# Attention slots of a two-layer trunk: the place of the division by the softmax sum, and of the convolution's taps

## The chip, the core and the metric

The kernel runs on one core of one Trainium2 chip, in one launch. The metric is the device time of an execution in microseconds. TensorE (PE) multiplies matrices and turns blocks, VectorE (DVE), ScalarE (ACT) and GpSimd (POOL) work on elements, and SyncE (SP) starts the transfers of the weights. Every engine has its own queue and works through it in the order of the program; semaphores tie the queues together. An instruction that waits holds up all that stands behind it in its queue.

## What is computed

Two layers, each with token mixing in three branches, a LayerNorm, and a SwiGLU network with a second LayerNorm, for 512 tokens of 1024 numbers in float32. Cut to what matters here:

```python
h = x @ w_in                                    # split into column groups
# branch A: 8 heads, one shared key; a light indexer picks 128 keys of each query
s = (q . k) * scale; s = where(selected, s, -inf)
y_a = softmax(s) @ v
# branch B: 8 heads with keys of their own, causal softmax over 512 keys
y_b = softmax(where(causal, (q . k) * scale, -inf)) @ v
# branch C: a causal depthwise convolution of width 31 over 512 channels
h = conv(a * sigmoid(g), width=31) + conv_b; y_c = silu(layer_norm(h))
gates = sigmoid(gate_pre + b_gate)              # 3 x 1024 columns of x @ w_in
merged = gates[0]*(y_a @ wb[0]) + gates[1]*(y_b @ wb[1]) + gates[2]*(y_c @ wb[2])
x = layer_norm(ALPHA * x + merged @ w_out)
```

## The kernel before, in words

A product in float32 is made of three: every operand is split into a high part, rounded to the format that TensorE takes, and a low part, the remainder, and high times high, high times low and low times high are summed. ScalarE makes the high part as a copy, VectorE or GpSimd the low part as a difference. That holds for the weights (`high` at L526 on ScalarE, `low` at L453 on GpSimd) and for everything inside attention.

The change touches one stretch of each layer, the function `attention`, which every engine has in its own version. It works through 64 *units* in a layer (`UNITS`), a unit being one head and one block of 128 queries. Units 0 to 31 are branch B, 32 to 63 branch A. Unit n has n mod 4 as its query block, and its scores are 128 times that block plus one wide, so 128, 256, 384 or 512 columns. The masked scores of unit n lie in `pbuf[n % 3]`. Time is cut into *slots*. In slot s:

- TensorE makes the scores of unit s (`score`, L962 to L970), turns the probabilities of unit s - 2 block by block (`turn`, L936), and in every second slot multiplies two turned units by the values (`value`, L986). Between these it works on the projections of the three gates: 24 weight tiles of eight *parts* (three products of 512 columns each, L829 to L831), dealt evenly over the slots by `attention_steps`. A turn waits for `prob_ready`.
- VectorE masks the scores and takes their extreme (`mask`, L1283), makes the reciprocal of a unit's sum (`inverse`, L1290), adds two halves of a value product (`combine`, L1305, odd slots), and takes the low part of the turned probabilities (`turned_lows`, L1297), for which it waits for ScalarE's copy of the same block. Beside these it has the 124 *taps* of the convolution (4 blocks of channels by 31, L1315 to L1321), each a pass over 512 columns that adds to a PSUM bank, and in slots 0 to 11 two of the selection steps of branch A (L1265, L1267). The table `TAPS_AT` says how many taps a slot has. The first tap of a slot stands ahead of `turned_lows`, all others behind it.
- ScalarE makes the exponential of unit s with its sum (`exponentials`, L564), divides (`probabilities`, L571: it multiplies by the reciprocal), copies turned probabilities out of PSUM (`turned_probabilities`, L580), copies half a value product (`value_part`, L587), makes the sigmoid of a finished gate tile (`gate`, L530, at a tile's last part) and the high part of a coming weight tile (L526, at a tile's first part). Some slots (`PREP`) hold the preparation of a head: two turned copies (L552, L553, or L556 and L558). Slot 8 has the copies of the shared key and value (L613, L614), slots 57 to 60 one copy each of the finished branch B (L621).

The order of each queue is written out by hand: ScalarE and TensorE walk over the same list `STEPS`, VectorE has its own loop over the slots. In ScalarE's walk, the step ("turn", s - 2) of slot s holds three instructions: the copy of unit s - 2, the exponential of unit s, the division of unit s - 1. In VectorE's loop a slot begins with the mask of unit s, and the reciprocal of unit s - 1 follows.

Of the kernel before, what the change touches and what calls it, by code (L numbers as in the profile page):

```python
# [108 lines left out]
UNITS = 2 * AH * NT  # L109
# [7 lines left out]
Y_SPLIT = {57 + c: c for c in range(4)}  # L117
KA_SLOT = 8
# [4 lines left out]
KEEP_SLOT = len(SELECT_LATE) // 2  # L123
TAPS_AT, _taps = [], 0
for _slot in range(UNITS):
    _n = 1 if _slot <= KEEP_SLOT else 3 if (_slot - KEEP_SLOT) % 5 == 4 else 2
    TAPS_AT.append(range(_taps, min(_taps + _n, CK * CW)))
    _taps = TAPS_AT[-1].stop
assert _taps == CK * CW
# [109 lines left out]
def build(nc, x_t, ple_t, pos, freq, weights, params, out):  # L239
    with ExitStack() as ctx:  # L240
# [270 lines left out]
        def _(act):  # L511
# [20 lines left out]
            def attention(layer, first):  # L532
# [57 lines left out]
                for kind, n in STEPS:  # L590
                    if kind == "part" and n[1] == 0:
                        high(T_GATE + n[0] + LEAD, first)
                    elif kind == "part" and n[1] == DK - 1:
                        g, j = GATE_ORDER[n[0]]
                        gate(T_GATE + n[0], first, 6 + n[0] % 2, gate_at(g, j), column("bg", g * DK + j), gate_done)
                    elif kind == "rope":
                        rope_keys()
                    elif kind == "prep":
                        prepare(n)
                    elif kind == "turn":  # L600
                        turned_probabilities(n)
                        if n + TURN_LAG < UNITS:
                            exponentials(n + TURN_LAG)
                        if n + 1 < UNITS:
                            probabilities(n + 1)
                    elif kind == "score" and n < TURN_LAG:
                        exponentials(n)
                        if n == 1:
                            probabilities(0)
                    elif kind == "value":  # L610
                        value_part(n)
                    elif kind == "slot" and n == KA_SLOT:
                        nc.scalar.activation(ka_h[:], ka_t[:], ACT.Copy).then_inc(ka_high, 1)  # L613
                        nc.scalar.activation(idx_r[:, :, G_VA - AD:G_VA], h_idx[:, :, G_VA:G_VA + AD],  # L614
                                             ACT.Copy).then_inc(va_high, 1)
                    elif kind == "slot" and n in Y_SPLIT:
                        c = Y_SPLIT[n]
                        if c == 0:
                            act.wait_ge(turn_out, turns + (TURN_AT[("prep", ("A", 3), "")] + 1))
                            act.wait_ge(value_out, layer * PAIRS + PAIRS // 2)  # L620
                        nc.scalar.activation(yh[1][:, c], yb[:, c], ACT.Copy).then_inc(y_high, 1)  # L621
# [43 lines left out]
            for layer in range(L):  # L665
# [87 lines left out]
                for q in range(12):  # L753
# [8 lines left out]
                    if q >= 8:  # L762
                        for c in range(2):
                            n = 2 * (q - 8) + c
# [423 lines left out]
        def _(dve):  # L1188
# [80 lines left out]
            def attention(layer, last_conv_input):  # L1269
# [84 lines left out]
                steps.wait()  # L1354
                last_conv_input()
                for slot in range(UNITS + NORM_LAG):
                    if slot < UNITS:
                        mask(slot)
                    if 1 <= slot <= UNITS:
                        inverse(slot - 1)  # L1360
                    if slot >= NORM_LAG and (slot - NORM_LAG) % 2:
                        combine((slot - NORM_LAG) // 2)
                    taps = list(TAPS_AT[slot]) if slot < UNITS else []
                    late = SELECT_LATE[2 * slot:2 * slot + 2]
                    for k in taps[:1]:
                        tap(k)
                    for step in late[:1]:
                        select(step, back=0)
                    if slot in PREP:
                        lows("prep", PREP[slot])  # L1370
                    if TURN_LAG <= slot < UNITS + TURN_LAG:
                        turned_lows(slot - TURN_LAG)
                    for k in taps[1:]:
                        tap(k)
                    for step in late[1:]:
                        select(step, back=0)
                    if KEEP_SLOT <= slot < KEEP_SLOT + NT - 1:
                        qt = slot - KEEP_SLOT + 1
                        span = slice(wide(qt), wide(qt) + width(qt))
                        steps.wait()  # L1380
                        steps.done(v.tensor_scalar(keep_bias[:, span], work[:, span], -2e38, NEG, ALU.is_gt, ALU.mult))
                    if slot == KA_SLOT:
                        dve.wait_ge(ka_high, layer + 1)
                        v.tensor_tensor(ka_l[:], ka_t[:], ka_h[:].bitcast(F32), ALU.subtract).then_inc(ka_ready, 1)
                        dve.wait_ge(va_high, layer + 1)
                        v.tensor_tensor(idx_r[:, :, G_VA:G_VA + AD], h_idx[:, :, G_VA:G_VA + AD],
                                        idx_r[:, :, G_VA - AD:G_VA].bitcast(F32), ALU.subtract).then_inc(va_low, 1)
# [412 lines left out]
```

## Time and profile before

| | us |
|---|---|
| median of 3 runs | 1850.85 |
| lowest and highest run | 1849.95, 1851.07 |
| the profiled execution, whole | 1852.88 |
| its span, first to last instruction | 1851.1 |
| TensorE busy | 1811.0 |
| VectorE busy | 1065.1 |
| ScalarE busy | 813.2 |
| GpSimd busy | 771.2 |

The profile is of one execution; times in it count from its first instruction. Matmuls overlap in the queue, and their ends are modelled, so TensorE counted as busy may still lose time; its weight loads (PEld) are the better sign of a wait. "Idle before" an instruction is the time for which its engine did nothing, with the engine, tile and line whose signal ended it. Where two instructions of one engine overlap by some 0.1 us, the next has begun while the end of the last is still being written. The attention stretch of the first layer runs from about 157 to 373 us, that of the second from about 1073 to 1289 us.

### The profile page before, as it was taken

The page shows a single profiled execution, that of the slowest core. Times are in us where ns is not written, and L with a number is a line of the kernel's source. Part 1 is how long each engine was busy: PE and PEld are TensorE (multiplying, and loading weights), DVE is VectorE, ACT ScalarE, POOL GpSimd, SP SyncE. Part 2 cuts the span into 40 slices and gives each one's busy share as a digit, 9 for nine tenths or more (in the row PEclk, how much of TensorE's full clock was granted, in tenths as well). Part 3 has the DMA queues.
Part 4 walks back from the last instruction along what each step waited for, and adds up shares of the span by engine and source line. Part 5 has one row for each costly group of instructions (what it writes and reads, how often), then busy time and mean ns, then how long its engine had stood idle before and what let it go on. Part 6 is the DMA issues. An engine that isn't in the chain of part 4 may idle for free.

```text
span 1851.1 us, 25182 instructions
## 1 busy us (share of the span) xinstructions
PE 1811.0 (98%) x8654; PEld 1502.9 (81%) x8654; DVE 1065.1 (58%) x1965; ACT 813.2 (44%) x1431; POOL 771.2 (42%) x336
## 2 busy tenths in 40 slices
PE   9999999999999999999999999999999999999997
PEld 9887787878778888888897877888887888888885
DVE  6379999868973111203254999997889711111033
ACT  4544777743433232322244457777434322322222
POOL 5443223345354444444444522233543544444541
PEclk9999999999999999999999999999999999999998
DMA  5322111223233332333333321122232332333331
GB/s 185 103 95 88 46 58 58 70 69 103 82 112 102 91 101 92 101 103 103 101 95 91 108 75 46 58 64 63 83 103 79 112 100 93 94 99 101 103 103 57
DMA packets 47032, 166.04 MB, mean 90 GB/s; under 512 B 5472, under 2 KB 5728, under 8 KB 46944
## 3 DMA queue, kind: packets, MB, share of 16 engines
q1 hardware_dynamic: 46080, 163.60, 28.3%
q10 hardware_dynamic: 864, 1.28, 0.2%
q8 instruction: 54, 0.88, 0.2%
q14 instruction: 34, 0.28, 0.0%
HBM read 162.76 MB, written 2.10 MB: 89 GB/s over the span
## 4 chain that ended last, share of the span: by engine, by line
PE 69%; issue 12%; DVE 9%; POOL 5%; ACT 4%; DMA 0%; DVEq 0%; POOLq 0%; ACTq 0%; SPq 0%
PE banks L829 18%; PE banks L831 18%; PE banks L830 18%; POOL sb_wl L453 4%; PE banks L880 3%; PE banks L882 3%; PE banks L881 3%; PE banks L936 2%; PE banks L986 2%; DVE sb_work L1267 1%; DVE sb_top L1265 1%; ACT sb_pbuf L564 1%; ACT sb_pbuf L571 1%; ACT sb_wh L526 1%; DVE banks L1319 1%
## 5 line engine op out<-in xcount | busy, mean ns | idle before, releaser
L453 POOL TENSOR_TENSOR sb_wl<-sb_wraw,sb_wh 128x1024 fp32r<-128x1024 f32 x303 | 743.8, 2458 | 1039.1 <-ACT sb_wh L526 1038.8
L829 PE MATMUL banks<-sb_xh,sb_wh 128*128 128x512 f32 x1344 | 540.6, 402 | 2.8 <-POOL sb_wl L453 1.8
L831 PE MATMUL banks<-sb_xh,sb_wl 128*128 128x512 f32 x1344 | 525.1, 391 | 0.0
L830 PE MATMUL banks<-sb_xl,sb_wh 128*128 128x512 f32 x1344 | 524.3, 390 | 0.0
L526 ACT ACTIVATE sb_wh<-sb_wraw 128x1024 fp32r<-128x1024 f32 x303 | 319.6, 1055 | 281.3 <-PE banks L831 175.1
L831 PEld LDWEIGHTS banks<-sb_xh,sb_wl 128*128 128x128 f32 x1344 | 252.2, 188 | 54.5
L829 PEld LDWEIGHTS banks<-sb_xh,sb_wh 128*128 128x128 f32 x1344 | 253.2, 188 | 52.9 <-issue 5.1
L830 PEld LDWEIGHTS banks<-sb_xl,sb_wh 128*128 128x128 f32 x1344 | 253.2, 188 | 41.3
L1319 DVE SCALAR_TENSOR_TENSOR banks<-sb_hconv,sb_par,banks 128x512 f32<-128x512 f32 x232 | 172.2, 742 | 1.5
L829 PE MATMUL banks<-sb_hh,sb_wh 128*128 128x512 f32 x352 | 137.7, 391 | 0.0
L831 PE MATMUL banks<-sb_hh,sb_wl 128*128 128x512 f32 x352 | 137.0, 389 | 0.0
L830 PE MATMUL banks<-sb_hl,sb_wh 128*128 128x512 f32 x352 | 137.0, 389 | 0.0
L1690 DVE TENSOR_TENSOR sb_th<-sb_th,banks 128x512 f32<-128x512 f32 x44 | 30.2, 687 | 175.8 <-PE banks L831 175.8
L1687 DVE SCALAR_TENSOR_TENSOR sb_th<-sb_th,banks 128x512 f32<-128x512 f32 x44 | 30.2, 687 | 158.2 <-ACT sb_th L530 158.2
L805 ACT ACTIVATE sb_hh<-sb_th 128x512 f32 x44 | 27.8, 633 | 204.4 <-DVE sb_th L1690 204.4
L530 ACT ACTIVATE sb_th<-banks 128x512 f32<-128x512 f32 x60 | 35.8, 597 | 175.3 <-PE banks L831 170.8
L1401 DVE TENSOR_TENSOR sb_u<-sb_u,banks 128x512 f32<-128x512 f32 x32 | 21.8, 687 | 151.4 <-PE banks L831 150.9
L880 PE MATMUL banks<-sb_wh,sb_xh 128*128 128x452 f32 (+3 forms) x256 | 89.3, 349 | 0.5 <-DVE sb_xl L1490 0.5
L881 PE MATMUL banks<-sb_wl,sb_xh 128*128 128x452 f32 (+3 forms) x256 | 89.1, 348 | 0.0
L882 PE MATMUL banks<-sb_wh,sb_xl 128*128 128x452 f32 (+3 forms) x256 | 89.0, 348 | 0.0
L564 ACT ACTIVATE sb_pbuf<-sb_pbuf,sb_small 128x128 f32<-128x128 f32 (+3 forms) x128 | 71.5, 559 | 37.3 <-DVE sb_small L1283 36.8
L830 PEld LDWEIGHTS banks<-sb_hl,sb_wh 128*128 128x128 f32 x352 | 66.1, 188 | 14.2 <-issue 0.5
(294 smaller groups left out, 2936.3 us busy)
## 6 DMA issues: line engine op xcount, KB each, us to landing
sb_wraw<-in_weights SPq DMA_DIRECT2D x304, 512.0 KB, 3.6
sb_u<-in_x SPq DMA_DIRECT2D x8, 256.0 KB, 6.3
out<-sb_u SPq DMA_DIRECT2D x8, 256.0 KB, 2.0
sb_praw<-in_ple ACTq DMA_DIRECT2D x2, 512.0 KB, 4.3
sb_par<-in_params ACTq DMA_DIRECT2D x2, 98.5 KB, 2.5
sb_rope_tmp<-in_freq ACTq DMA_DIRECT2D x1, 24.0 KB, 4.4
sb_small<-in_pos ACTq DMA_DIRECT2D x1, 2.0 KB, 4.1
```

The source lines that it names most:

```text
L453: nc.gpsimd.tensor_tensor(wl[:, t % WS, :], wraw[:, t % 2, :], wh[:, t % WS, :].bitcast(F32), ALU.subtract).then_inc(lo_ready, 1)
L526: nc.scalar.activation(wh[:, t % WS, :], wraw[:, t % 2, :], ACT.Copy).then_inc(hi_ready, 1)
L564: nc.scalar.activation(pbuf[:, n % 3, 0:w], pbuf[:, n % 3, 0:w], ACT.Exp, scale=-1.0, bias=nmax[:, n % 4:n % 4 + 1], accum_out=psums[:, n ...
L829: nc.tensor.matmul(out, wh_, xh_, start=start, stop=False)
L830: nc.tensor.matmul(out, wh_, xl_, start=False, stop=False)
L831: return nc.tensor.matmul(out, wl_, xh_, start=False, stop=stop)
L880: nc.tensor.matmul(o, th_, h[:, kk], start=(k == 0), stop=False)
L881: nc.tensor.matmul(o, th_, lw[:, kk], start=False, stop=False)
L882: last = nc.tensor.matmul(o, tl_, h[:, kk], start=False, stop=(k == GROUP_K[name] - 1))
L936: last = nc.tensor.transpose(psum[0:rows, bank, b * P:b * P + P], src, ident[:])
L986: last = nc.tensor.matmul(psum[:, bank, q0:256], v, pt[half][:, b, q0:256], start=(i == 0), stop=(i == len(passes) - 1))
L1319: steps.done(v.scalar_tensor_tensor(acc, h, w, acc, ALU.mult, ALU.add))
```

## The change

On ScalarE the division of unit s - 1 no longer follows the exponential of unit s; it is now the first instruction of slot s. On VectorE the reciprocal of unit s - 1 now stands ahead of the mask of unit s. Since the branch for the step "slot" is now taken by the division, the two branches for slot 8 and slots 57 to 60 become ifs of their own and follow it. And the taps are dealt by another table: slots 0 to 12 keep one; up to slot 31 a slot has two, or one where its number is 4 modulo 5; from slot 32 on it has two, or three where its number is 0 or 2 modulo 5.

```diff
--- before.py
+++ after.py
@@ -123,7 +123,10 @@
 KEEP_SLOT = len(SELECT_LATE) // 2
 TAPS_AT, _taps = [], 0
 for _slot in range(UNITS):
-    _n = 1 if _slot <= KEEP_SLOT else 3 if (_slot - KEEP_SLOT) % 5 == 4 else 2
+    if _slot < UNITS // 2:
+        _n = 1 if _slot <= KEEP_SLOT or _slot % 5 == 4 else 2
+    else:
+        _n = 3 if _slot % 5 in (0, 2) else 2
     TAPS_AT.append(range(_taps, min(_taps + _n, CK * CW)))
     _taps = TAPS_AT[-1].stop
 assert _taps == CK * CW
@@ -601,19 +604,17 @@
                         turned_probabilities(n)
                         if n + TURN_LAG < UNITS:
                             exponentials(n + TURN_LAG)
-                        if n + 1 < UNITS:
-                            probabilities(n + 1)
                     elif kind == "score" and n < TURN_LAG:
                         exponentials(n)
-                        if n == 1:
-                            probabilities(0)
                     elif kind == "value":
                         value_part(n)
-                    elif kind == "slot" and n == KA_SLOT:
+                    elif kind == "slot" and 1 <= n <= UNITS:
+                        probabilities(n - 1)
+                    if kind == "slot" and n == KA_SLOT:
...
-                    elif kind == "slot" and n in Y_SPLIT:
+                    if kind == "slot" and n in Y_SPLIT:
                         c = Y_SPLIT[n]
                         if c == 0:
...
@@ -1354,10 +1355,10 @@
                 steps.wait()
                 last_conv_input()
                 for slot in range(UNITS + NORM_LAG):
+                    if 1 <= slot <= UNITS:
+                        inverse(slot - 1)
                     if slot < UNITS:
                         mask(slot)
-                    if 1 <= slot <= UNITS:
-                        inverse(slot - 1)
```

What the queues look like. The first place is ScalarE in slots 55 and 56 (the copy of unit 53, in two blocks, opens the piece). L580 is the copy of the turned probabilities, L564 the exponential, L571 the division, L530 the gate, L526 the weight copy, L587 half a value product; widths tell the units apart: 512 is unit 55, 384 unit 54, 128 unit 56. Before:

```order
L580 ACTIVATE sb_pt_h_90<-banks 128x2x128
L564 ACTIVATE sb_pbuf,sb_small<-sb_pbuf,sb_small 128x512
L571 ACTIVATE sb_pbuf<-sb_pbuf,sb_small 128x384
L530 ACTIVATE sb_gb<-banks,sb_par 128x512
L580 ACTIVATE sb_pt_h_91<-banks 128x3x128
L564 ACTIVATE sb_pbuf,sb_small<-sb_pbuf,sb_small 128x128
L571 ACTIVATE sb_pbuf<-sb_pbuf,sb_small 128x512
L526 ACTIVATE sb_wh<-sb_wraw 128x1024
L587 ACTIVATE sb_low_part<-banks 64x256
```

After, the same place (all line numbers here are 3 higher):

```order
L574 ACTIVATE sb_pbuf<-sb_pbuf,sb_small 128x384
L583 ACTIVATE sb_pt_h_90<-banks 128x2x128
L567 ACTIVATE sb_pbuf,sb_small<-sb_pbuf,sb_small 128x512
L574 ACTIVATE sb_pbuf<-sb_pbuf,sb_small 128x512
L533 ACTIVATE sb_gb<-banks,sb_par 128x512
L583 ACTIVATE sb_pt_h_91<-banks 128x3x128
L567 ACTIVATE sb_pbuf,sb_small<-sb_pbuf,sb_small 128x128
L529 ACTIVATE sb_wh<-sb_wraw 128x1024
L590 ACTIVATE sb_low_part<-banks 64x256
```

The division of unit 55 (512 columns) has moved from behind the exponential of unit 56 to the front of slot 56, ahead of the gate and of the copy of unit 54.

The second place is VectorE in slots 50 and 51: L1283 is the mask (the row with 128x1 reads its extreme out), L1290 the reciprocal, L1319 a tap and L1321 the last one of a block of channels, L1297 the low part. Before:

```order
L1283 ISA sb_pbuf,sb_small<-banks,sb_work 128x384
L1283 ISA sb_small 128x1
L1290 RECIPROCAL sb_small<-sb_small 128x1
L1319 SCALAR_TENSOR_TENSOR banks<-sb_hconv,sb_par,banks 128x512
L1297 TENSOR_TENSOR sb_pt_l_92<-banks,sb_pt_h_90 128x128
L1319 SCALAR_TENSOR_TENSOR banks<-sb_hconv,sb_par,banks 128x512
L1283 ISA sb_pbuf,sb_small<-banks,sb_work 128x512
```

After (line numbers 1 higher):

```order
L1291 RECIPROCAL sb_small<-sb_small 128x1
L1284 ISA sb_pbuf,sb_small<-banks,sb_work 128x384
L1284 ISA sb_small 128x1
L1320 SCALAR_TENSOR_TENSOR banks<-sb_hconv,sb_par,banks 128x512
L1298 TENSOR_TENSOR sb_pt_l_92<-banks,sb_pt_h_90 128x128
L1320 SCALAR_TENSOR_TENSOR banks<-sb_hconv,sb_par,banks 128x512
L1322 SCALAR_TENSOR_TENSOR sb_hconv<-sb_hconv,sb_par,banks 128x512
L1291 RECIPROCAL sb_small<-sb_small 128x1
```

The reciprocal has moved ahead of the mask, and this slot has three taps instead of two, two of them in a row behind the low part.

The third place is ScalarE in slot 8, where L613 and L614 (before) are the copies of the shared key and value. Before:

```order
L564 ACTIVATE sb_pbuf,sb_small<-sb_pbuf,sb_small 128x512
L571 ACTIVATE sb_pbuf<-sb_pbuf,sb_small 128x384
L613 ACTIVATE sb_ka_h<-sb_ka_t 128x512
L614 ACTIVATE sb_idx_r<-sb_h_idx 128x4x64
L580 ACTIVATE sb_pt_h_91<-banks 128x3x128
```

After:

```order
L567 ACTIVATE sb_pbuf,sb_small<-sb_pbuf,sb_small 128x512
L574 ACTIVATE sb_pbuf<-sb_pbuf,sb_small 128x512
L614 ACTIVATE sb_ka_h<-sb_ka_t 128x512
L615 ACTIVATE sb_idx_r<-sb_h_idx 128x4x64
L583 ACTIVATE sb_pt_h_91<-banks 128x3x128
```

The division between the exponential of unit 7 and the key copies is now that of unit 7 itself, which waits for VectorE to begin slot 8.

## Rows read from the trace of the kernel before

**Rows 1.** The page, its first part: busy time, share of the span, instructions.

```profile
PE 1811.0 (98%) x8654; PEld 1502.9 (81%) x8654; DVE 1065.1 (58%) x1965; ACT 813.2 (44%) x1431; POOL 771.2 (42%) x336
```

**Rows 2.** Stretches between masks 0, 13, 32, 63: PE, PEld, DVE, ACT, POOL busy.

```profile
167.60:210.50 42.90, 40.07 (x224) 32.89 (x224) 40.66 (x116) 32.06 (x76) 11.92 (x5) 1.00 0.17 50
210.50:272.80 62.30, 61.37 (x347) 51.65 (x347) 58.68 (x145) 46.36 (x111) 14.38 (x6) 1.00 0.18 60
272.80:364.40 91.60, 89.77 (x494) 74.12 (x494) 85.03 (x214) 72.52 (x171) 26.13 (x12) 1.00 0.19 58
```

**Rows 3.** Waits over the whole program: us in total, times, longest us.

```profile
PEld banks L936 <- ACT sb_pbuf L571: 21.4, 37, 1.3
```

**Rows 4.** Waits, two rows of 272.8 to 369.6, then one of 210.5 to 272.8.

```profile
PEld banks L936 <- ACT sb_pbuf L571: 6.6, 12, 1.0
DVE sb_pbuf L1283 <- PE banks L970: 3.7, 6, 1.2
...
PEld banks L936 <- ACT sb_pbuf L571: 1.8, 4, 0.5
```

**Rows 5.** Timeline, 290 to 302: start, us, engine, line, operation, idle before.

```profile
293.91 0.38 ACT L587 ACTIVATE sb_low_part<-banks 64x256 f32<-64x256 f32 x1
294.32 0.42 DVE L1305 TENSOR_TENSOR sb_ya<-banks,sb_low_part 64x256 f32<-64x256 f32 x1 [0.27 <-ACT sb_low_part L587]
...
294.60 0.71 ACT L564 ACTIVATE sb_pbuf<-sb_pbuf,sb_small 128x512 f32<-128x512 f32 x1
...
295.30 0.60 ACT L571 ACTIVATE sb_pbuf<-sb_pbuf,sb_small 128x384 f32<-128x384 f32 x1
295.32 0.41 DVE L1297 TENSOR_TENSOR sb_pt_l<-banks,sb_pt_h 128x256 fp32r<-128x256 f32 x1
295.66 0.74 DVE L1319 SCALAR_TENSOR_TENSOR banks<-sb_hconv,sb_par,banks 128x512 f32<-128x512 f32 x1
295.96 0.31 PEld L936 LDWEIGHTS banks<-sb_ident,sb_pbuf 128*128 128x128 f32 x3 [0.54 <-ACT sb_pbuf L571]
...
296.31 0.28 DVE L1283 CUSTOM_DVE_ANT_0 sb_pbuf<-banks,sb_causal 128x128 f32<-128x128 f32 x1
...
296.52 0.15 DVE L1290 RECIPROCAL sb_small<-sb_small 128x1 f32<-128x1 f32 x1
...
296.60 0.73 DVE L1319 SCALAR_TENSOR_TENSOR banks<-sb_hconv,sb_par,banks 128x512 f32<-128x512 f32 x1
...
301.20 1.54 DVE L1319 SCALAR_TENSOR_TENSOR banks<-sb_hconv,sb_par,banks 128x512 f32<-128x512 f32 x2
```

**Rows 6.** ScalarE's instructions by shape, 272.8 to 364.4: busy, mean ns.

```profile
L571 ACT ACTIVATE sb_pbuf<-sb_pbuf,sb_small 128x512 f32<-128x512 f32 x8 | 5.7, 714 | 0.0
L530 ACT ACTIVATE sb_gb<-banks,sb_par 128x512 f32<-128x512 f32 x8 | 5.5, 688 | 5.9 <-PE banks L831 5.9
...
L580 ACT ACTIVATE sb_pt_h<-banks 128x384 fp32r<-128x384 f32 x8 | 3.9, 484 | 1.9 <-PE banks L936 1.9
```

**Rows 7.** Lines 613 and 614: duration ns least, median, most.

```profile
L613 ACT ACTIVATE sb_ka_h<-sb_ka_t x2: 614/615/616, 191.8 to 1107.7; 128x512 fp32r<-128x512 f32 x2
...
L614 ACT ACTIVATE sb_idx_r<-sb_h_idx x2: 402/402/402, 192.3 to 1108.3; 128x256 fp32r<-128x256 f32 x2
```

**Rows 8.** Timeline at slot 13, the turn of unit 11.

```profile
211.44 0.63 PE L936 MATMUL banks<-sb_ident,sb_pbuf 128*128 128x128 f32 x4 [0.80 <-DVE sb_yb L1305]
```

**Rows 9.** Timeline: score 32, mask 32, score 63, mask 63, turn 63.

```profile
270.38 0.19 PEld L969 LDWEIGHTS banks<-sb_ka_h,sb_q_h 128*128 128x128 f32 x1
...
272.83 0.28 DVE L1283 CUSTOM_DVE_ANT_0 sb_pbuf<-banks,sb_causal 128x128 f32<-128x128 f32 x1
...
363.37 0.19 PEld L969 LDWEIGHTS banks<-sb_ka_h,sb_q_l 128*128 128x128 f32 x1
...
364.45 0.69 DVE L1283 CUSTOM_DVE_ANT_0 sb_pbuf<-banks,sb_work 128x512 f32<-128x512 f32 x1 [0.54 <-PE banks L970]
...
369.52 0.14 PEld L936 LDWEIGHTS banks<-sb_ident,sb_pbuf 128*128 128x128 f32 x1
```

## The prediction

> **What bounds the kernel now.** I read the page's busy times first, then busy time by stretch, then the waits, and last the timeline of a few microseconds of the stretch that the change touches. TensorE is busy for 98% of the span and VectorE for 58% [rows 1]. That is an average over stages: the change touches only the attention stretch (about 157 to 373 us in the first layer, the same again from 1073 us in the second), and the windows there read differently. I cut the stretch at three masks: unit 0 to unit 13, unit 13 to unit 32, unit 32 to unit 63. VectorE is busy for 40.66 of 42.90 us, 58.68 of 62.30 and 85.03 of 91.60 [rows 2]. So two engines are nearly full at once, and each waits a little for the other. TensorE's wait for the division `probabilities` (L571 on ScalarE) is 21.4 us in 37 pieces over both layers [rows 3]; in the first layer 6.6 of it lies behind unit 32 and 1.8 between units 13 and 32 [rows 4]. VectorE waits 3.7 us for scores behind unit 32 [rows 4].
>
> How a division comes late can be followed at unit 38 [rows 5]: the exponential of unit 39 starts at 294.60, the division of unit 38 stands behind it and starts at 295.30, and its turn on TensorE starts at 295.96, after 0.54 us of idle weight loading. Had the division stood ahead of unit 39's mask and exponential, it would have been done more than a microsecond earlier.
>
> All terms below are for one layer, and both layers are alike in these windows; the sum is doubled at the end.
>
> **Part 1, the new place of division and reciprocal.** No instruction is added. On VectorE the reciprocal (0.16 us, it takes 0.08 of the queue) changes places with a mask. VectorE's own queue gets no longer, so this costs it nothing as long as the exponential of the unit before is done when the slot begins; in the stretch shown the exponential of unit 39 ends at 295.3 and the next slot's mask starts at 296.3 [rows 5]. What it gives: a division is ready about 0.2 + 0.7 us after VectorE begins a slot, where it now takes mask, exponential and division, some 2.1 us. The single waits of TensorE for L571 are at most 1.3 us [rows 3], so I take all of them as gone. If nothing came in their place the gain would be 21.4 us less some 0.05 us of ordinary gap in each of the 37: 19.5 us for both layers, 9.8 for one.
>
> What is queued behind the moved wait: on ScalarE the division now stands at the head of the slot and waits for VectorE to begin that slot. Behind it stand the head copies of `prepare`, a gate, and the copy L580 of the unit two before, for which VectorE itself waits in the same slot (L1297). Before, that copy stood ahead of the exponential's wait and was mostly done when VectorE came. This is a new ring: VectorE begins, reciprocal, division, copy, VectorE's L1297. Its length against VectorE's own way to L1297, from the moment a slot begins, for a slot whose number is a multiple of four: ScalarE needs 0.20 (reciprocal and signal), 0.62 (division of 512 columns, 0.71 with its last 0.1 under the next instruction), 0.48 (copy of 384) and 0.03 (from a ScalarE end to a waiting VectorE start, as at 294.32), so 1.33 us; VectorE needs 0.08, 0.21 (mask of 128 columns), 0.08 and 0.65 (one tap), so 1.02 us [rows 5, 6]. VectorE would wait 0.31 us. The other three kinds of slot have 0.4 to 0.7 us to spare, because the mask is wider or a `combine` comes between. A gate ahead of the copy adds 0.6 us [rows 6]; behind unit 32 that is in every third slot, where it makes 0.9 us of wait at slots 44 and 56 and 0.2 at slots 38, 41, 50 and 62. With 0.3 in each of the six other multiples of four and some 1.5 us for the copies of `yb` in slots 57 to 60 (L621, as long as a gate), the sum is 6 us if VectorE is the late engine throughout, and nothing where it still waits for scores. I take 4.0 us: late most of the time, as part 2 shows, but not in the first slots behind unit 32. The ends are 0 and 6. One more place: slot 8 puts the key copies of L613 and L614 (0.6 and 0.4 us of the queue [rows 7]) between division and copy. By the same count the copy ends at 2.2 us and VectorE comes at 1.5, so 0.7 us, between 0 and 1.
>
> **Part 2, the taps.** The number stays 124. Counted from the two tables, slots 0 to 31 get 47 instead of 55, slots 32 to 62 get 75 instead of 68 and slot 63 two instead of one; slots 0 to 13 keep their numbers. A tap alone holds the queue for 0.65 us (from 295.66 to the mask at 296.31); two in a row last 1.54, so with 0.75 for the second the first holds it for 0.79, since the next tap waits for its sum [rows 5]. A third tap is always such a one, so seven more cost 5.5 us between the masks of units 32 and 63, and the busy time there goes from 85.0 to 90.5 [rows 2].
>
> In the section "The DRAIN you can't avoid" of the page "VectorE: DVE Perf Modes" the Trainium skill says that a semaphore between two VectorE operations costs nothing extra. By that, a tap behind a tap would take 0.65 too and the term would be 4.6 us; the rows show 0.79, and I keep them.
>
> **The sum for one layer.** Units 0 to 13: VectorE idles 2.2 of 42.9 us [rows 2], so it is the bound already, and TensorE is tied to it at slot 13, where it waits 0.80 us for the `combine` of the same slot [rows 8]. Waits that go from TensorE ahead of that point come back there: gain 0, and 0.7 lost at slot 8. Units 14 to 31: VectorE loses eight taps, 6.3 us of work, and is no longer late; TensorE sets the pace and gains its own waits there, 1.3 us (four for L571, the one at unit 32 left out, and a short one for `combine`; between 0.5 and 1.5). Units 32 to 63 on VectorE: 90.5 busy, 1.0 of small gaps that stay (of 6.6, the 3.7 for scores go), 4.0 of the new ring: 95.5 instead of 91.6, so plus 3.9. Two corrections at the ends. The mask of unit 32 stood 2.45 us behind its score [rows 9]; relieved of eight taps it should follow at about 1.2 (at unit 63, where VectorE waited for the score, it was 1.08 [rows 9]): minus 1.2. At the end, unit 63's turn came 5.07 us after its mask [rows 9]; with VectorE late it can follow after mask, combine, two taps, L1297, reciprocal and division, about 3.9: minus 1.1. Together 0.7 - 1.3 + 3.9 - 1.2 - 1.1 = plus 1.0 us, 2.0 us for both layers. The profiled execution took 1852.88 us, 2 us over the median of the runs; the difference goes on the median: 1850.85 + 2.0 is about **1853 us**.
>
> The bounds of that sum: with ring 0, slot 8 at 0, gaps of 0.4, taps at 0.65 and 1.5 gained before unit 32 one layer comes to minus 5.4, so 1840; with ring 6, a full microsecond at slot 8 and 0.5 gained before unit 32 to plus 4.1, so 1859.
>
> **The rivals.**
> 1. Nothing takes the waits' place. If VectorE had room behind unit 32, TensorE would win all of its waits: 1850.85 - 19.5 = about 1831 us. For it: 98% TensorE on the page [rows 1]. Against it: VectorE's 90.5 us of work alone, beside some 86 us that TensorE needs there (91.6 less its waits of 6.6 there, with their ordinary gaps). Chance 0.08.
> 2. VectorE is the bound, but the ring costs next to nothing, since ScalarE had 19 of 91.6 us free [rows 2]. TensorE can then run further ahead of VectorE than now and evens out the slots: ring 0 to 1, so minus 2 to 3 us a layer and around 1845 us, with 1841 to 1849 as its own range. Chance 0.20. The Trainium skill points at this bound: in "Perfetto Trace Analysis", section "Identifying the Most-Contended Engine", it takes occupancy as the measure for Vector and calls matmul busy time a bad one. By that rule VectorE is the engine to relieve, and no change that leaves its work as it is wins TensorE's waits; the windows' 85.03 of 91.60 agree.
> 3. Slower: the ring through ScalarE. It decides once VectorE is late in nearly all slots behind 32, so that the 6 us (or more, with the exponential and a weight copy behind it also coming late in gate slots) are paid in full: plus 3 to 6 us for one layer, 1857 to 1863 us. For it: 2.92 us of VectorE work in a mean slot behind unit 32 (90.5 over 31) against 2.78 for TensorE (86 over 31). It is the change's own price: more taps where TensorE has the shorter slots. Chance 0.27.
> 4. The change doesn't do what it says: VectorE falls so far behind (3 us) that divisions still come late. TensorE would go on waiting for L571, at VectorE's pace as now: 1851 us. Chance 0.07.
>
> **How the numbers follow.** The likeliest case, both engines trading small waits, has 0.38 and by itself 1849 to 1857. About 0.2% (3.7 us) is what a measurement of this kernel can tell from no change, so the borders are 1847.1 and 1854.6. Faster: rival 1 with 0.08 and most of rival 2 with 0.17, so 0.25. Slower: rival 3 with 0.27 and 0.10 of the likeliest case, so 0.37. Within: 0.38. The range reaches into rivals 2 and 3 and leaves rival 1 and some 0.08 more out: 1841 to 1861.
>
> **What would show it.** In the changed kernel's profile TensorE's waits for L574 (the division's new line) should be under 2 us in each attention stretch; if they are not, rival 4. Behind unit 32 VectorE should be busy for some 90.5 us between the masks of units 32 and 63, its waits for scores should nearly vanish, and it should wait for the copy L583 by 3 to 5 us in a layer, most of it in slots that are multiples of four. Under 1 us of that is rival 2, over 6 rival 3. TensorE's waits should have moved to VectorE's results: L1298 at the value products, L1306 at the turns, or the masks at the scores. Between units 14 and 31 VectorE should wait for scores by 4 us or more. The prediction is wrong at its root if VectorE behind unit 32 is idle by over 4 us while the time falls.

## The result, and the profile after

| | before | after |
|---|---|---|
| median of 6 runs, us | 1850.93 | 1861.03 |
| lowest and highest, us | 1849.82, 1851.15 | 1860.08, 1861.93 |
| the profiled execution, its span, us | 1852.88, 1851.1 | 1861.0, 1859.2 |

The changed kernel is slower: ratio 1.0055, 95% interval 1.0044 to 1.0066, which is 10.1 us. The forecast was 1853 with 1841 to 1861 as its range, so the time lies 0.03 us outside its upper edge, and on the side of rival 3.

The page's first part, its answer to [rows 1], shows nothing of it. The engines do the same work in a span 8.1 us longer (the profiled execution of the kernel before took 1852.88 us, 2 us over its median, so the two spans differ by less than the medians):

```profile
PE 1811.8 (97%) x8654; PEld 1501.4 (81%) x8654; DVE 1066.0 (57%) x1965; ACT 812.1 (44%) x1431; POOL 771.4 (41%) x336
```

The same three stretches as in [rows 2], again cut at the masks of units 0, 13, 32 and 63 (window, length, then busy time of PE, PEld, DVE, ACT, POOL; granted clock, DMA share, GB/s):

```profile
167.45:210.22 42.77, 39.83 (x222) 32.52 (x223) 40.01 (x116) 30.87 (x74) 11.96 (x5) 1.00 0.16 50
210.22:270.99 60.77, 60.71 (x349) 52.02 (x348) 53.39 (x139) 46.58 (x111) 14.39 (x6) 1.00 0.20 60
270.99:370.60 99.61, 93.16 (x502) 75.03 (x501) 90.74 (x223) 72.98 (x172) 26.30 (x13) 1.00 0.18 54
```

The granted clock is 1.00 in all of them, as before. The first stretch is 0.1 us shorter, the second 1.5 us shorter, the third 8.0 us longer. In the third VectorE's work rose from 85.03 to 90.74 us, by 5.7; the other 2.3 us are more idle time of VectorE (8.87 us, where it was 6.57), although it had become the late engine.

The end of the layer's stretch, in answer to [rows 9] (timeline: start, duration, engine, line; a weight load of score 32, mask 32, a weight load of score 63, mask 63, turn 63):

```profile
269.31 0.19 PEld L970 LDWEIGHTS banks<-sb_ka_h,sb_q_h 128*128 128x128 f32 x1
...
270.99 0.26 DVE L1284 CUSTOM_DVE_ANT_0 sb_pbuf<-banks,sb_causal 128x128 f32<-128x128 f32 x1
...
368.39 0.19 PEld L970 LDWEIGHTS banks<-sb_ka_h,sb_q_l 128*128 128x128 f32 x1
...
370.60 0.67 DVE L1284 CUSTOM_DVE_ANT_0 sb_pbuf<-banks,sb_work 128x512 f32<-128x512 f32 x1
...
374.37 0.59 PEld L937 LDWEIGHTS banks<-sb_ident,sb_pbuf 128*128 128x128 f32 x4
```

Mask 32 follows its score by 1.68 us (2.45 before), mask 63 by 2.2 us although nothing was left to wait for, and turn 63 comes 3.77 us after its mask (5.07 before). So the layer, from mask 0 to turn 63, reads as follows, in us; "forecast" is the sum of the prediction, with the correction for the lag of mask 32 put into the second stretch, where it falls:

| stretch | before | after | difference | forecast |
|---|---|---|---|---|
| mask 0 to mask 13 | 42.85 | 42.78 | -0.07 | +0.7 |
| mask 13 to mask 32 | 62.35 | 60.76 | -1.59 | -1.3 - 1.2 |
| mask 32 to mask 63 | 91.62 | 99.61 | +7.99 | +3.9 |
| mask 63 to turn 63 | 5.06 | 3.78 | -1.28 | -1.1 |
| sum | 201.88 | 206.93 | +5.05 | +1.0 |

The second layer gives 207.14 - 202.07 = +5.07. Together that is 10.1 us, as much as the medians differ by; the 2 us that the profiled execution of before took over its median lie outside these stretches. The third row holds most of the miss.

The waits in that row's stretch (engine, tile and line waited for: us in total, times, longest), in answer to [rows 4]:

```profile
ACT sb_pbuf L574 <- DVE sb_small L1291: 26.3, 23, 2.6
PEld banks L987 <- DVE sb_idx_r L1298: 7.9, 7, 1.7
...
DVE sb_idx_r L1298 <- ACT sb_pt_h L583: 4.6, 9, 1.1
PEld banks L937 <- ACT sb_pbuf L574: 3.1, 6, 0.8
...
DVE sb_q_h L1338 <- ACT sb_q_l L556: 1.2, 3, 0.4
...
DVE sb_pt_l L1298 <- ACT sb_pt_h L583: 0.6, 3, 0.2
...
DVE sb_pbuf L1284 <- PE banks L971: 0.3, 1, 0.3
```

Everyone waits for VectorE: ScalarE's division 26.3 us for the reciprocal, TensorE's value products 7.9 us for the low part. VectorE waits for scores by 0.3 us where it was 3.7, so it has next to no slack left. What it waits for instead is ScalarE: 4.6 + 0.6 us for the copy L583 (0.7 us in the kernel before), and 1.2 us for a copy of `prepare` (before, none). These 6.4 us lie in the queue of the engine that sets the time.

In the stretch before it, masks 13 to 32, the change did what it was to do: VectorE, relieved of taps, waits for scores by 4.8 us, and TensorE's waits for the division fell from 1.8 to 0.5.

```profile
DVE sb_pbuf L1284 <- PE banks L965: 4.8, 7, 1.1
...
PEld banks L937 <- ACT sb_pbuf L574: 0.5, 1, 0.5
```

### The profile page after: what moved, and what is told of

Same layout as the page of the kernel before. It is cut to its first block, busy times and chain, and to the rows that moved or that the text cites. A ratio compares the mean times of both kernels' runs of the same rounds, so it can differ in the third digit from the quotient of the medians.

```text
span 1859.2 us, 25182 instructions
## 1 busy us (share of the span) xinstructions
PE 1811.8 (97%) x8654; PEld 1501.4 (81%) x8654; DVE 1066.0 (57%) x1965; ACT 812.1 (44%) x1431; POOL 771.4 (41%) x336
## 3 DMA queue, kind: packets, MB, share of 16 engines
q10 hardware_dynamic: 864, 1.28, 0.2%
## 4 chain that ended last, share of the span: by engine, by line
PE 65%; issue 14%; DVE 13%; POOL 5%; ACT 4%; DMA 0%; DVEq 0%; POOLq 0%; ACTq 0%; SPq 0%
PE banks L830 17%; PE banks L832 17%; PE banks L831 17%; POOL sb_wl L456 4%; DVE banks L1320 3%; PE banks L881 3%; PE banks L883 3%; PE banks L882 3%; PE banks L937 1%; PE banks L987 1%; DVE sb_work L1268 1%; DVE sb_top L1266 1%; DVE sb_pbuf L1284 1%; ACT sb_wh L529 1%; DVE sb_idx_r L1298 1%
```

## The ring, seen in one slot

Slot 44 is a multiple of four, its mask is the narrow one, and it has a gate. VectorE in slot 44 of the changed kernel, from the reciprocal to the next slot's (the bracket is the idle time before the row and what ended it):

```profile
308.82 0.15 DVE L1291 RECIPROCAL sb_small<-sb_small 128x1 f32<-128x1 f32 x1
308.89 0.27 DVE L1284 CUSTOM_DVE_ANT_0 sb_pbuf<-banks,sb_causal 128x128 f32<-128x128 f32 x1
...
309.09 0.75 DVE L1320 SCALAR_TENSOR_TENSOR banks<-sb_hconv,sb_par,banks 128x512 f32<-128x512 f32 x1
310.71 0.56 DVE L1298 TENSOR_TENSOR sb_idx_r<-banks,sb_pt_h 128x384 fp32r<-128x384 f32 x1 [0.88 <-ACT sb_pt_h L583]
311.19 0.75 DVE L1320 SCALAR_TENSOR_TENSOR banks<-sb_hconv,sb_par,banks 128x512 f32<-128x512 f32 x1
311.85 0.15 DVE L1291 RECIPROCAL sb_small<-sb_small 128x1 f32<-128x1 f32 x1
```

ScalarE in the same slot:

```profile
309.01 0.72 ACT L574 ACTIVATE sb_pbuf<-sb_pbuf,sb_small 128x512 f32<-128x512 f32 x1 [1.44 <-DVE sb_small L1291]
309.64 0.67 ACT L533 ACTIVATE sb_gb<-banks,sb_par 128x512 f32<-128x512 f32 x1
310.20 0.48 ACT L583 ACTIVATE sb_pt_h<-banks 128x384 fp32r<-128x384 f32 x1
```

VectorE begins the slot at 308.82. ScalarE had been idle for 1.44 us and can start the division only then, at 309.01; the gate and the copy stand behind it, the copy starts at 310.20 and ends at 310.68. VectorE has been through with its tap since 309.83 and stands still for 0.88 us. It does not help that VectorE was late when the slot began: ScalarE's chain starts with VectorE's slot, so it is always late by the same amount. That is why the waits of the changed kernel come out nearly slot by slot as the two queues were counted in the prediction: 0.30 in slots 32, 36, 40, 48 and 52, 0.88 in 44 and 56, 0.13, 0.19 and 0.18 in 38, 50 and 62, and 1.6 us together in slots 57, 59 and 60. Only in slot 41, where 0.2 was counted, is there none.

## Experiments

Times are medians; ratios are to the kernel before, run beside them (1850.51 us, 22 runs, for the first four; 1849.98 us, 12 runs, for the others; 1850.93 us beside the changed kernel). Since these differ by up to 0.95 us, a difference between kernels of different groups is given also by their traces, as the time from mask 0 to turn 63, over both layers. In the kernel before that is 201.88 + 202.07 us, in the changed one 206.93 + 207.14.

### 1. The new order with the old taps

```diff
-    if _slot < UNITS // 2:
-        _n = 1 if _slot <= KEEP_SLOT or _slot % 5 == 4 else 2
-    else:
-        _n = 3 if _slot % 5 in (0, 2) else 2
+    _n = 1 if _slot <= KEEP_SLOT else 3 if (_slot - KEEP_SLOT) % 5 == 4 else 2
```

> The new order of division and reciprocal with the old table of taps. Theory A (two prices add up behind unit 32: seven more taps of 0.79 us, and the ring in which VectorE's low part waits for a copy that stands behind a division that waits for VectorE): the ring stays and the taps' price goes. VectorE between the masks of units 32 and 63 is busy 85 us and waits about 5 us for the copy, so that stretch is 91 to 94 us instead of 99.6; between units 13 and 32 it is about 61.5, at the tail 3.8. About plus or minus 1 us a layer against the kernel before: 1848 to 1853 us. Theory B (the order alone is the cost, whatever the taps): 1857 us or more. Theory C (the taps alone are the cost, the order gives what it was to give): 1840 us or less, and waits for the copy under 1 us.

Measured: 1855.89 us, ratio 1.0033 (1.0021 to 1.0046), which lies between the bands of theories A and B. It is slower than before with not one tap moved: the order alone costs 5.4 us. Its stretch behind unit 32 (line numbers 3 lower than in the changed kernel: L1295 is the low part, L580 the copy):

```profile
273.27:367.51 94.24, 90.58 (x498) 75.02 (x498) 85.22 (x216) 72.00 (x171) 26.15 (x12) 1.00 0.18 57
```

```profile
DVE sb_idx_r L1295 <- ACT sb_pt_h L580: 5.1, 9, 1.1
...
DVE sb_q_h L1335 <- ACT sb_q_l L553: 1.2, 3, 0.4
...
DVE sb_pt_l L1295 <- ACT sb_pt_h L580: 0.8, 4, 0.2
```

VectorE has 85.22 us of work, as before, and 94.24 us pass. The waits for ScalarE are there all the same, 7.1 us (6.4 in the changed kernel): they hang on the order in the queues and not on the taps. TensorE's waits for the division are not in the list any more, and VectorE's for scores neither, and yet the stretch is 2.6 us longer than before. Theory A had the ring right and its price too low: VectorE waited 5.9 us for the copy where 5 were expected, another 1.2 us for `prepare`, and the stretch between masks 13 and 32 took 63.2 us where 61.5 were expected (62.35 before).

### 2. The new taps with the old order

The same edit the other way round, in the kernel before.

> The new table of taps with the old order. Theory A: VectorE is busy 90.5 us behind unit 32 and has next to no waits for the copy, so that stretch is 93 to 95 us; TensorE still waits for the division; between units 13 and 32 the time falls by 1 to 2 us. 1852 to 1857 us. Theory B: 1851 us or less. Theory C: 1858 us or more, since nothing of the order's gain is there to set against the taps.

Measured: 1852.40 us, ratio 1.0012 (1.0002 to 1.0022), within the expectation. The stretch behind unit 32 takes 93.98 us with 89.72 of VectorE's work, so 2.4 more than before, and 1.2 us come back between masks 13 and 32 (61.12). The taps alone cost 1.9 us, with an interval from 0.4 to 4.1, hardly more than can be told from nothing.

### 3. Copy first, then the division, then the exponential

In the kernel before, ScalarE's step `turn` gets the order copy of unit s - 2, division of unit s - 1, exponential of unit s; VectorE has the reciprocal ahead of the mask, as in the changed kernel. The division is as early as it can be without standing ahead of the copy.

```diff
                     elif kind == "turn":
                         turned_probabilities(n)
-                        if n + TURN_LAG < UNITS:
-                            exponentials(n + TURN_LAG)
                         if n + 1 < UNITS:
                             probabilities(n + 1)
+                        if n + TURN_LAG < UNITS:
+                            exponentials(n + TURN_LAG)
...
                 for slot in range(UNITS + NORM_LAG):
-                    if slot < UNITS:
-                        mask(slot)
                     if 1 <= slot <= UNITS:
                         inverse(slot - 1)
+                    if slot < UNITS:
+                        mask(slot)
```

> A third order with the old taps: on VectorE the reciprocal ahead of the mask, on ScalarE copy of unit s-2, division of unit s-1, exponential of unit s. The division still comes ahead of the exponential, but the copy no longer stands behind it, so the ring is open. Theory A: waits for the copy as few as in the kernel before (under 1.5 us between units 32 and 63), TensorE's waits for the division mostly gone, VectorE no more the late engine: that stretch 87 to 90 us, 1840 to 1846 us in all. Theory B (any order that makes ScalarE wait for the reciprocal earlier costs): no faster than 1850 us. Theory C: like the order-only kernel within 2 us.

Measured: 1842.30 us, ratio 0.996 (0.9946 to 0.9974), 8.2 us faster than before and within theory A's 1840 to 1846. Behind unit 32 VectorE's waits for scores have fallen from 3.7 to 1.5 us, TensorE's for the division from 5.9 (up to mask 63) to 0.9, and VectorE's wait for a copy comes once:

```profile
271.30:360.24 88.94, 88.65 (x492) 74.40 (x492) 84.57 (x215) 72.62 (x170) 26.15 (x12) 1.00 0.20 60
```

```profile
DVE sb_pbuf L1283 <- PE banks L970: 1.5, 2, 0.8
...
PEld banks L936 <- ACT sb_pbuf L571: 0.9, 4, 0.3
...
DVE sb_idx_r L1297 <- ACT sb_pt_h L580: 0.6, 1, 0.6
```

### 4. Copy first with the new taps

> The third order (copy, division, exponential) with the new taps. Theory A: the difference to the changed kernel is the ring alone, 5 to 7 us a layer behind unit 32: that stretch 92 to 94 us, 1846 to 1851 us in all. Theory B: within 3 us of the changed kernel, 1858 us or more. Theory C (taps alone): the same as the changed kernel, 1859 to 1862 us.

Measured: 1845.79 us, ratio 0.9977 (0.9968 to 0.9987), 0.2 us below theory A's 1846 to 1851. This kernel differs from the changed one only in ScalarE's order: the copy stands ahead of the division, and the ring is open. The stretch behind unit 32:

```profile
269.91:362.16 92.25, 91.19 (x500) 75.23 (x499) 89.43 (x223) 74.03 (x172) 26.68 (x13) 1.00 0.20 58
```

92.25 us against 99.61, with the same taps in the same slots. Of the 7.36 us between them, 6.05 are idle time of VectorE (8.87 against 2.82) and 1.31 busy time. And slot 44 on VectorE, to be held against the slot above:

```profile
305.95 0.16 DVE L1293 RECIPROCAL sb_small<-sb_small 128x1 f32<-128x1 f32 x1
...
306.22 0.75 DVE L1322 SCALAR_TENSOR_TENSOR banks<-sb_hconv,sb_par,banks 128x512 f32<-128x512 f32 x1
306.88 0.55 DVE L1300 TENSOR_TENSOR sb_idx_r<-banks,sb_pt_h 128x384 fp32r<-128x384 f32 x1
307.35 0.75 DVE L1322 SCALAR_TENSOR_TENSOR banks<-sb_hconv,sb_par,banks 128x512 f32<-128x512 f32 x1
308.00 0.16 DVE L1293 RECIPROCAL sb_small<-sb_small 128x1 f32<-128x1 f32 x1
```

From reciprocal to reciprocal it takes 2.05 us, where the changed kernel takes 3.03. That is 0.98 more, for a wait of 0.88. The other 0.10 us is the overlap: here each operation starts about 0.1 us before the end of the one before it (the tap of 0.75 us holds the queue for 0.66), and an operation that stands behind a wait has none.

### 5. Two taps ahead of the low part

In the changed kernel VectorE does two taps ahead of the low part instead of one, so that the copy has time to come.

```diff
-                    for k in taps[:1]:
+                    for k in taps[:2]:
                         tap(k)
...
-                    for k in taps[1:]:
+                    for k in taps[2:]:
                         tap(k)
```

> The changed kernel, with the second tap of each slot moved ahead of the low part on VectorE too. The ring is left as it is, but VectorE now comes 0.79 us later to the place where it waits for the copy. Theory A (the ring costs because the copy is late against VectorE's own way): the waits for the copy behind unit 32 fall from 5.2 us to about 1 in the first layer (slots 57 to 60 are left), the stretch between the masks of units 32 and 63 from 99.6 to 93 to 95 us, 1848 to 1852 us in all. Rival (VectorE's waits for the copy are a symptom, and the time is lost because divisions and low parts reach TensorE late): TensorE gets the low part another 0.8 us later, so no faster than 1859 us.

Measured: 1857.47 us, ratio 1.0039 (1.0024 to 1.0053): 3.6 us less than the changed kernel (3.5 by the traces), and between the two expectations, so it bears out neither in full.

```profile
271.36:367.83 96.47, 91.53 (x497) 74.51 (x496) 91.54 (x223) 72.77 (x171) 26.17 (x12) 1.00 0.18 56
```

```profile
DVE sb_ya L1306 <- ACT sb_low_part L590: 1.9, 3, 0.7
...
DVE sb_idx_r L1298 <- ACT sb_pt_h L583: 0.4, 1, 0.4
```

The waits for the copy fell from 5.2 to 0.4 us, as the theory of the ring says. Two things ate most of the gain. The first is a pair of taps where there was none. A tap that follows a tap doesn't overlap it, since it needs its sum, so the first holds the queue for 0.79 instead of 0.66 us. In slot 46, which has two taps, the pair and the low part behind it are:

```profile
317.23 1.54 DVE L1320 SCALAR_TENSOR_TENSOR banks<-sb_hconv,sb_par,banks 128x512 f32<-128x512 f32 x2
318.68 0.28 DVE L1298 TENSOR_TENSOR sb_pt_l<-banks,sb_pt_h 128x128 fp32r<-128x128 f32 x1
```

From its mask to the next the slot takes 2.18 us, where it takes 2.05 in experiment 4. Slots with three taps had such a pair already, behind the low part, and take the same time in both (2.84 us in slots 40, 42, 50 and 52). So the pair is new in the 18 slots of two taps alone, and 18 by 0.13 is 2.3 us. The second is a new wait, 1.9 us for ScalarE's half of a value product, which experiment 4 doesn't have. From experiment 4's 92.25 us these two lead to 96.5; measured were 96.47. Why that half comes late here was not followed.

### 6. The changed kernel with the mask ahead of the reciprocal

```diff
                 for slot in range(UNITS + NORM_LAG):
-                    if 1 <= slot <= UNITS:
-                        inverse(slot - 1)
                     if slot < UNITS:
                         mask(slot)
+                    if 1 <= slot <= UNITS:
+                        inverse(slot - 1)
```

> The changed kernel with VectorE's old order: mask, then reciprocal. ScalarE still has the division at the head of the slot. That puts the mask (0.21, 0.34, 0.47 or 0.61 us of the queue) into the ring. Theory A, by the same count as for the changed kernel: 0.52 us of wait in multiples of four without a gate (six), 1.1 with one (two), 0.5 to 0.7 in the other gate slots (seven), 0.1 in the rest of the kind 2 modulo 4, and about 2.4 in slots 57 to 60: 11 to 13 us in a layer behind unit 32 instead of 5 to 6. 1871 to 1876 us. Rival (the cost is not this ring): within 3 us of the changed kernel, 1858 to 1864 us.

Measured: 1879.71 us, ratio 1.016 (1.0143 to 1.0177). The ring is now longer by a mask in every slot:

```profile
DVE sb_idx_r L1298 <- ACT sb_pt_h L583: 6.4, 10, 1.2
...
DVE sb_pt_l L1298 <- ACT sb_pt_h L583: 4.4, 7, 0.8
...
DVE sb_q_h L1338 <- ACT sb_q_l L556: 1.9, 3, 0.7
```

That is 10.8 us for the copy and 1.9 for `prepare`, 12.7 where 11 to 13 were expected. The wait in a plain multiple of four went from 0.30 to 0.52, by the 0.2 us for which its narrow mask holds the queue. The stretch behind unit 32 grew by 6.75 us (waits by 6.3). The time is 3.7 us over the expectation's upper end, for which the waits had been counted only behind unit 32: 1.1 us more per layer came ahead of unit 13, and 1.4 between 13 and 32. This is the strongest run for the ring: one instruction of 0.16 us, moved by one place, changes the time by 18.7 us (19.2 by the traces), where it changes it by 1.8 (2.1 by the traces) without the ring (experiment 7).

### 7. Copy first with the mask ahead of the reciprocal

Experiment 3 with VectorE's old order: ScalarE's half of it alone.

> ScalarE: copy, division, exponential. VectorE: mask, then reciprocal, as before the change. Old taps. Only ScalarE's half of the third order. Theory A: no ring, since the copy stands ahead of both waits; the division comes 0.3 to 0.6 us later than with the reciprocal first and takes the exponential with it. Waits of TensorE for the division come back in part. 1843 to 1847 us. Rival (the gain of the third order comes from VectorE's half): 1849 us or more.

Measured: 1844.10 us, ratio 0.9968 (0.9958 to 0.9979), within theory A's 1843 to 1847. So without the ring the place of the reciprocal hardly matters: 1.8 us, with intervals that overlap. Most of the gain over before, 5.9 of 8.2 us, lies in the division standing ahead of the exponential.

### 8. Copy first, with taps taken from the slots where VectorE is late

In experiment 3 the slots up to 13 have VectorE as their bound, and behind them it still waits for scores at times. Three taps go from slots 5, 8 and 9 to slots 14, 18 and 24.

```diff
-    _n = 1 if _slot <= KEEP_SLOT else 3 if (_slot - KEEP_SLOT) % 5 == 4 else 2
+    if _slot <= KEEP_SLOT:
+        _n = 0 if _slot in (5, 8, 9) else 1
+    else:
+        _n = 3 if (_slot - KEEP_SLOT) % 5 == 4 or _slot in (14, 18, 24) else 2
```

> The third order (reciprocal ahead of the mask; copy, division, exponential) with a table of taps by where VectorE is late: none in slots 5, 8 and 9, three in slots 14, 18 and 24, else the old table. Theory A (each engine's pace in each stretch decides): slots 0 to 13 are VectorE's, and three taps less shorten that stretch by about 2 us; slots 14, 18 and 24 have room, since VectorE waits for scores there. 1 to 2 us less a layer: 1838 to 1841 us. Rival (only the total of VectorE's work counts): 1842 us as the third order with the old taps.

Measured: 1839.91 us, ratio 0.9947 (0.993 to 0.9963), the lowest median of all and within theory A's 1838 to 1841; its interval overlaps that of experiment 3, so the gain over that kernel rests on the traces. In the first layer mask 0 to 13 fell from 42.66 to 41.09 us and 13 to 32 rose from 61.71 to 62.45, 0.8 us in all; both layers together, up to turn 63, give 2.0 of the 2.4 us.

### The prices together

| ScalarE in a slot | old taps | new taps |
|---|---|---|
| copy, exponential, division (before) | 1850.5 | 1852.4 |
| division, copy, exponential (after) | 1855.9 | 1861.0 |
| copy, division, exponential | 1842.3 | 1845.8 |

The ring, middle row against last row, costs 13.6 us with the old taps and 15.2 with the new, several times what the intervals leave to noise. The new taps cost 1.9 us under the old order, 5.1 under the changed one and 3.5 with the copy first. The intervals of these three differences overlap, but the traces, with one execution each, give nearly the same (2.0, 5.1 and 3.5 us), so it looks as if the two prices don't simply add up.

## Why the prediction was wrong

**What bounds the kernel: right.** Two engines nearly full behind unit 32, each waiting a little for the other, was the reading of [rows 2] and [rows 4]. In experiment 3, where both wait less, the time falls by 8.2 us.

**No instruction more: right. The waits for the division went, but not all.** Over both layers they fell from 21.4 us in 37 pieces [rows 3] to 12.6 in 23:

```profile
PEld banks L937 <- ACT sb_pbuf L574: 12.6, 23, 1.3
```

The step "I take all of them as gone" was too generous, and so was the sign set for it, under 2 us in each attention stretch: some 6 are left in each. Ahead of unit 13, where VectorE is late, the waits stayed (2.4 us in the first layer, 2.2 before); and behind unit 32 3.1 us are left. The division now waits for a VectorE whose mask starts up to 4.5 us behind the first weight load of its score (slots 38, 46, 54 and 58), which fits rival 4's mechanism, in a small part; experiment 4 has 2.3 us of these waits in the same stretch without the ring, so not all of the 3.1 is of this kind.

**The ring: its place and its waits right, its price wrong.** This is the step that failed: "I take 4.0 us: late most of the time [...] but not in the first slots behind unit 32". Of the hand count of 6 us 5.2 stand in the trace (4.6 + 0.6 us), and VectorE was late nearly from slot 32 on: the full 0.30 stands at slots 32, 36 and 40, and its waits for scores are 0.3 us. Two things were not in the count at all. One is the copies of `prepare`, which stand behind the division too: 1.2 us. The other is the overlap that an operation loses when it stands behind a wait, 0.1 us each time; VectorE's busy time is 90.74 us in the changed kernel and 89.43 in experiment 4 with the same operations. By experiment 4 the ring costs 99.61 - 92.25 = 7.36 us in this stretch, not 4.0. That is 3.36 of the miss of 4.05 us a layer.

**The taps: the price in the queue right, the agreement in busy time luck.** 85.0 + 5.5 = 90.5 us of work was forecast and 90.7 measured, but 1.3 of the 90.7 is the lost overlap that the ring brings. Without the ring the seven more taps add 4.7 us of busy time (experiment 2, 89.72) or 4.9 (89.43 in experiment 4 against 84.57 in experiment 3), not 5.5. That a tap in front of a tap holds the queue for 0.79 us stands: in experiment 5 a plain slot that gets such a pair is 0.13 us longer. The sentence of the Trainium skill that the prediction weighed there ("VectorE: DVE Perf Modes", section "The DRAIN you can't avoid", that a semaphore between two VectorE operations costs nothing extra, measured there on copies) doesn't hold for a tap that needs the sum of the one before it: with the next operation independent it holds the queue for 0.66 us, with the next one waiting for it for 0.79.

**The rest of the miss: 0.7 us a layer, in four pieces that partly cancel.** With the ring open the stretch behind unit 32 takes 92.25 us (experiment 4) where 90.5 + 1.0 was the base of the sum, 0.75 more: the work is 1.1 less, but VectorE idles 2.8 us and not 1.0. Masks 13 to 32 gave 1.6 us and not 2.5, since the lag of mask 32 shrank by 0.8 and not by 1.2, and the rest gained 0.8 and not 1.3. Against these stand slot 8, which lost nothing of its 0.7, and the end, which gained 1.3 for 1.1.

**Slot 8: the wait came, the loss didn't.** VectorE waits 0.35 us there and 0.31 in slot 12, yet mask 13 stands where it stood. The last section has what made up for it.

**The rivals.** Rival 3 happened, with its mechanism and in its own range (1857 to 1863); the point from which it decides, VectorE late in nearly all slots, was named, and so was the row that spoke for it (2.92 us of VectorE's work in a mean slot against 2.78 of TensorE's). An engine with more work in the mean slot than its partner doesn't work its lateness off: the mask of unit 32 already stood 1.68 us behind its score, where it can follow at 1.08 [rows 9], and but for slot 35, where VectorE catches up and waits 0.34 us for a score, the masks behind it stand 1.7 to 4.5 us behind their scores. Rival 2 is what the same taps take when the ring is open: about 1845 was said, and experiment 4 measured 1845.8, though that kernel has another order. The rule it drew, that no change which leaves VectorE's work as it is wins TensorE's waits, is refuted by experiment 7: the same work on VectorE, TensorE's waits for the division behind unit 32 down from 5.9 to 1.5 us, and 5.9 us gained. Its argument, that ScalarE had 19 us free, is where it misled. Free time of ScalarE is worth nothing when its queue starts by waiting for the engine that waits for it: of ScalarE's idle time in the changed kernel 26.3 us are exactly that.

## What to carry to other kernels

Before an instruction is moved to the front of an in-order queue, look what it waits for and what stands behind it: if it waits for engine A's current slot, and A waits in that slot for something behind it, the two queues have become a ring, and once A is late the wait is paid in full in every slot in which the second queue is the longer, however much idle time its engine has. Put what the bound engine waits for ahead of everything that waits for the bound engine. And work is best moved between stages by their paces: a stage in which an engine already has no wait for its partner pays for every added operation, at the price that the operation has beside its new neighbours (a tap in front of a tap holds the queue longer than a tap alone).

## What the runs showed of the hardware

VectorE's operation at L1381 (a tensor_scalar that writes what branch A may see, once for each of three query blocks) took very different times in its first, narrowest place, 256 columns in slot 12. Before, first GpSimd's low part of a weight tile, then VectorE:

```profile
208.03 2.38 POOL L453 TENSOR_TENSOR sb_wl<-sb_wraw,sb_wh 128x1024 fp32r<-128x1024 f32 x1 [9.06 <-ACT sb_wh L526]
```

```profile
209.16 1.40 DVE L1381 TENSOR_SCALAR sb_work<-sb_work 128x256 f32<-128x256 f32 x1
```

In the changed kernel (L1382):

```profile
207.69 2.39 POOL L456 TENSOR_TENSOR sb_wl<-sb_wraw,sb_wh 128x1024 fp32r<-128x1024 f32 x1 [8.05 <-ACT sb_wh L529]
```

```profile
209.56 0.67 DVE L1382 TENSOR_SCALAR sb_work<-sb_work 128x256 f32<-128x256 f32 x1
```

In both it ends 0.15 us after GpSimd's instruction (210.41 and 210.56; 210.08 and 210.23). So it does in both layers of the experiments: in experiment 6, where GpSimd's instruction ends at 210.63, it takes 1.05 us and ends at 210.77; in experiment 3, where GpSimd's ends at 209.45, 1.41 us, and at 209.60. Its two wider forms, 384 and 512 columns, which had no GpSimd instruction beside them, take 0.36 and 0.43 us. So it looks as if this operation can't finish while GpSimd's runs. The taps don't show it: in the changed kernel 232 of them took 734 to 759 ns each, wherever GpSimd stood. The changed kernel reaches this place 0.4 us later and spends 0.7 us less there, which pays for its waits in slots 8 and 12. That GpSimd is the cause was read from the traces and not tried by a run of its own, and why the taps are spared stays open.
